# A router on rows that are not yet normed, its norm and modulation folded into its weights

## The chip, the cores and the metric

One core of one Trainium2 chip. The time is device microseconds of one execution. PE is TensorE, DVE is VectorE, ACT is ScalarE, POOL is GpSimd, SP is the queue that issues most loads.

## The reference, cut to what matters

Two layers of a hybrid block (retention, dilated attention, a gated MLP) run first, then one second block on the same 256 tokens of width 1024: a state-space mixer beside a pooling branch, then a mixture of 32 experts of hidden size 512. What the change touches is the seam between mixer and experts:

```python
xl = post_norm(xl, mod_l[2] * out_l, ln1_g, ln1_b)   # layer_norm(ALPHA * x + y) * g + b
hl = modulate(xl, mod_l[3], mod_l[4])                # x * (1 + scale) + shift
lg = hl @ w_rg + b_rg                                # 4 groups; softmax, argmax
le = hl @ w_re + b_re                                # 8 experts in each; top 2 of the group
y  = sum over the 2 experts of weight * (silu(h @ wg) * (h @ wu)) @ wd
xl = post_norm(xl, mod_l[5] * y, ln2_g, ln2_b)
```

All of it is float32.

## The kernel before

Five instruction streams are written out by hand, one for each engine and one for SP; they are tied by semaphores through `at(key)` (wait) and `then(..., key)` (signal). The operations are recorded by helpers, so all products have line 143, turns (transposes) 145, activations 147, tensor_tensor 149, tensor_scalar 151, scalar_tensor_tensor (`stt`) 153, reductions 155, copies 159, bn_stats 165, bn_aggr 167, DMAs 169.

*Up to the router.* Products of the mixer use split operands: each fp32 operand is written as a rounded high and low part (type fp32r), and three rounded products (`mm3`) take the place of one fp32 product. The output product `o2` is done for token tile 0 first, then tile 1 (128 tokens each). `first_norm(i)` on DVE scales the two halves of 512 columns by `MG[:, 1]`, adds `ALPHA * X`, takes bn_stats, and calls `layer_norm`: mean and variance, POOL takes the root, DVE subtracts and scales into `X`, multiplies by the norm's gain row `GB[:, 0]`, and DVE and POOL add the bias row `GB[:, 1]`, a half each, writing `X` in an order in which column 4p + k stands at 128k + p (`in_fours`, `by_four`). The two rows are loaded by POOL (`norm_rows`), behind its last work of the mixer.

*The router.* PE turns `X` (four 128 x 128 blocks for each `hm(i, q)`), ACT (and DVE for one quarter) applies the modulation while copying into `HM`, and PE multiplies by `WR`, 36 columns (4 groups, 32 experts), in plain fp32. DVE adds the biases, finds greatest values and one-hot rows in a chain of small instructions up to `SEL`; `CW` holds the two weights of each token, `RK` its rank within each expert (a product with a triangle), `cnt` the greatest count, from which further rounds are decided.

*The experts.* They are taken two at a time, 16 pairs, 64 places for each expert of a pair. For pair p: `ones_of(p)` on DVE makes a one-hot `ONE` (token to place) and its weighted twin `PW`; `gather` multiplies rows of `X` by `ONE` into `HG`, with the modulation applied by DVE and ACT; two parts of gate/up products (fp32, 64 columns of weights, two experts side by side in the array); `AV = silu * up`; turns; `down` products; DVE scales by `MG[:, 0]` into `OE`; and `combine(p)`, which runs on PE between the two parts of gate/up of pair p + 1, multiplies the turned `PW` by `OE` in four fp32 products of 512 columns, which DVE adds to `YA`. Pair 0's addition also takes in `ALPHA * X`.

*The loads.* Each pair needs six loads of 2 MB (gate, up, down of two experts), numbered 0 to 95. There are nine slots; loads 0 to 7 are issued by ACT during the mixer's end, load 8 (its slot overlies the norm rows) by SP once the norm is over, and load k waits on SP until the products that read load k - 9 are done:

```python
y.wait_ge(*(at("gu", r, b, i // 2) if i < 4 else at("oe", r, b, 1)))
expert_load(y, r, k)
```

## Time and profile before

| | us |
|---|---|
| median of 3 runs | 1711.09 (1708.34 to 1715.6) |
| the profiled execution | 1707.69 |
| its span | 1705.8 |
| PE busy in the span | 1627.1 (95%) |
| DVE, ACT, POOL busy | 779.8, 584.7, 468.0 |
| mean granted clock of PE | 0.982 of full |
| moved by DMA | 397.84 MB, 233 GB/s over the span |

Busy time is a sum over stages with different limits: the experts' stage begins near 1224 us of the span and has another balance of products and loads than what is ahead of it. The rows below are read stage by stage. A granted clock of 1.00 is 2.4 GHz, 0.50 is 1.2 GHz. An fp32 product is recorded as two records, a rounded one as one.

### The profile page before, as it was taken

How to read it: one execution, taken by the hardware profiler on the slowest of the kernel's cores; microseconds unless marked ns; L12 is line 12 of the kernel's file. 1: busy time of each engine (PE TensorE's matmuls, PEld its weight loads, DVE VectorE, ACT ScalarE, POOL GpSimd, SP SyncE). 2: the span in 40 equal slices, each digit the busy share in tenths (PEclk: the TensorE clock that was granted, in tenths of full speed). 3: DMA queues.
4: the chain of work that ended last, by engine and by line, in shares of the span. 5: the costliest groups of instructions: out<-in, count | busy, mean ns of one | idle time of the engine just before them, and what ended most of it. 6: DMA issues, size and time to landing. Idle time of an engine off the chain costs nothing.

```text
span 1705.8 us, 23942 instructions
## 1 busy us (share of the span) xinstructions
PE 1627.1 (95%) x9717; PEld 1214.9 (71%) x9717; DVE 779.8 (46%) x1320; ACT 584.7 (34%) x1046; POOL 468.0 (27%) x297
## 2 busy tenths in 40 slices
PE   7999999999999999999999999998699999999996
PEld 5888998878879998888777888996444434344442
DVE  5644333246563332478856665455533323233224
ACT  4543444334443343555436565332200000000000
POOL 4532545433334444300035565343000000000000
PEclk9999999999999999999999999999699999999998
DMA  7644896536439886423213344956499999999992
GB/s 259 206 135 133 253 266 213 184 119 200 141 91 300 249 250 228 127 77 99 75 50 100 101 108 135 297 170 260 166 415 421 424 421 421 424 422 425 421 424 119
DMA packets 244196, 397.84 MB, mean 233 GB/s; under 512 B 6661, under 2 KB 195521, under 8 KB 223216
## 3 DMA queue, kind: packets, MB, share of 16 engines
q1 hardware_dynamic: 237360, 365.45, 61.6%
q10 hardware_dynamic: 3760, 20.85, 3.1%
q0 software_dynamic: 2960, 9.94, 1.7%
q8 instruction: 80, 1.31, 0.3%
q14 instruction: 36, 0.29, 0.1%
HBM read 395.16 MB, written 1.05 MB: 232 GB/s over the span
## 4 chain that ended last, share of the span: by engine, by line
PE 86%; DVE 7%; issue 3%; DMA 2%; POOL 2%; ACT 1%; ACTq 0%; DVEq 0%; POOLq 0%
PE ps L143 84%; DVE arena L153 2%; PE ps L145 2%; DVE arena L149 1%; DVE split_r L149 1%; DMA rows<-in_ln_b 1%; POOL split_r L149 1%; POOL small L169 1%; DMA ring<-in_w_in 1%; DMA X<-in_x 0%; ACT split_r L147 0%; ACT arena L147 0%; DVE X L153 0%; DVE arena L159 0%; POOL arena_r L149 0%
## 5 line engine op out<-in xcount | busy, mean ns | idle before, releaser
L143 PE MATMUL ps<-arena_r,split_r 128*128 128x256 f32 (+1 forms) x2984 | 462.2, 289 | 3.7 <-POOL split_r L149 3.7
L149 POOL TENSOR_TENSOR split_r<-ring,split_r 128x1024 fp32r<-128x1024 f32 (+1 forms) x142 | 334.6, 2358 | 330.0 <-ACT split_r L147 308.0
L143 PEld LDWEIGHTS ps<-arena_r,split_r 128*128 128x128 f32 x2984 | 395.7, 189 | 20.9 <-issue 15.7
L147 ACT ACTIVATE split_r<-ring 128x1024 fp32r<-128x1024 f32 (+1 forms) x293 | 296.0, 1019 | 301.7 <-PE ps L143 216.9
L143 PE MATMUL ps<-arena 128*64 128x512 f32 (+7 forms) x1472 | 359.5, 491 | 4.7 <-DVE arena L153 2.2
L149 DVE TENSOR_TENSOR split_r<-ring,split_r 128x1024 fp32r<-128x1024 f32 (+1 forms) x151 | 212.3, 1408 | 312.8 <-ACT split_r L147 305.0
L143 PE MATMUL ps<-split_r,arena_r 128*128 128x512 f32 (+1 forms) x1520 | 342.5, 378 | 2.7 <-issue 1.7
L143 PEld LDWEIGHTS ps<-split_r,arena_r 128*128 128x128 f32 x1520 | 274.7, 188 | 51.4 <-issue 7.5
L143 PEld LDWEIGHTS ps<-arena 128*64 128x64 f32 (+2 forms) x1472 | 153.5, 156 | 164.9 <-issue 147.4
L143 PE MATMUL ps<-hhh_r,split_r 128*128 128x256 f32 (+1 forms) x976 | 222.9, 317 | 0.0
L143 PE MATMUL ps<-ring,arena 128*64 128x512 f32 (+2 forms) x768 | 214.7, 584 | 4.4 <-DVE arena L149 2.4
L147 ACT ACTIVATE arena<-ps 128x256 f32<-128x256 f32 (+4 forms) x182 | 76.6, 435 | 335.3 <-PE ps L143 330.1
L149 DVE TENSOR_TENSOR arena<-arena,ps 128x512 f32<-128x512 f32 (+1 forms) x124 | 79.4, 640 | 235.3 <-PE ps L143 200.4
L143 PEld LDWEIGHTS ps<-hhh_r,split_r 128*128 128x128 f32 x976 | 163.1, 190 | 12.2 <-issue 0.7
L143 PEld LDWEIGHTS ps<-ring,arena 128*64 128x64 f32 (+1 forms) x768 | 76.4, 145 | 108.0 <-issue 96.5
L169 POOL DMA_DIRECT2D rows<-in_ln_g x2 | 1.2, 608 | 452.8 <-PE ps L143 452.8
L147 ACT ACTIVATE arena<-ps,modc 128x128 f32<-128x128 f32 x92 | 34.5, 457 | 248.0 <-PE ps L143 218.5
L149 DVE TENSOR_TENSOR arena<-ps,rows 128x512 f32<-128x512 f32 x60 | 40.7, 690 | 138.0 <-PE ps L143 137.5
L143 PEld LDWEIGHTS ps<-arena,X 128*128 128x128 f32 x640 | 77.3, 198 | 27.3 <-issue 23.8
L143 PE MATMUL ps<-arena,X 128*128 128x128 f32 x640 | 82.6, 284 | 13.5 <-DVE arena L151 13.5
L149 POOL TENSOR_TENSOR arena_r<-arena,arena_r 128x256 fp32r<-128x256 f32 (+1 forms) x46 | 38.2, 832 | 163.5 <-ACT arena_r L147 155.0
L153 DVE SCALAR_TENSOR_TENSOR arena<-ps,rows,arena 128x508 f32<-128x508 f32 (+4 forms) x104 | 69.7, 675 | 27.0 <-ACT arena L147 20.6
(147 smaller groups left out, 1164.5 us busy)
## 6 DMA issues: line engine op xcount, KB each, us to landing
ring<-in_w_gate_up SPq DMA_DIRECT2D x88, 512.0 KB, 7.4
arena<-in_w_expert_up SPq DMA_DIRECT2D x15, 2048.0 KB, 20.5
arena<-in_w_expert_gate SPq DMA_DIRECT2D x15, 2048.0 KB, 19.7
ring<-in_w_expert_down SPq DMA_DIRECT2D x15, 2048.0 KB, 21.8
ring<-in_w_in SPq DMA_DIRECT2D x57, 512.0 KB, 5.2
ring<-in_w_expert_gate SPq DMA_DIRECT2D x13, 2048.0 KB, 18.2
arena<-in_w_ada SPq DMA_DIRECT2D x24, 1024.0 KB, 7.4
ring<-in_w_down SPq DMA_DIRECT2D x22, 1024.0 KB, 5.0
```

What stands on the lines that cost most here:

```text
L143: made = e.matmul(*a, **k)
L145: made = e.transpose(*a, **k)
L147: made = e.activation(*a, **k)
L149: made = e.tensor_tensor(*a, **k)
L153: made = e.scalar_tensor_tensor(**k)
L169: made = e.dma_start(*a, **k)
```

## The change

The router works on `LT`, the sum before its norm, and the norm's mean and root come in afterwards, through the identity logits = rstd * (LT @ W') - mean * rstd * (column sums of W') + the rest, with W' = gain * (1 + scale) * W.

- PE: 16 products of 36 columns between `projected(1)` and `state_sum(3)` make the two constant rows `SC`, from the folded columns `mul = (1 + scale) * gain` and `add = shift + (1 + scale) * bias`, which DVE prepares at m = 12 of the convolution; DVE then stores `SC` and scales `WR`.
- `first_norm` writes `LT` in the order of fours and signals each half (`r`); PE turns it as soon as it is there, ACT copies without modulation, the logits of a tile have a bank of their own. ACT writes the normed rows (without gain and bias) into `X`; the modulation behind the gathering uses the folded columns.
- `layer_norm` goes from both engines. The gain and bias rows are loaded by POOL after `o2(1)` into `GROW` and `BROW`; POOL's `residual(i)` makes the residual's rows in `YA` after the first gathering, and pair 0's addition uses them.
- In the chain of small instructions, what waits for E4's exponential is moved behind `SEL`; the rank keeps its + 1 (the one-hot compares with 1 to 64); the rank's products are two instead of three; count and `cnt` come after the first gathering.
- In each pair: `PW` goes. PE turns `ONE` and gets the weight of each place by four fp32 products with one column; ACT copies them to `ONET` (rounded) and `WSL`. DVE multiplies the down products by `WSL` and `MG` at once into `OE`, ACT rounds that to `OEH`, DVE subtracts to `OEL`, and `combine` is two rounded products for each of the four fp32 ones. `OE` has one buffer.
- SP issues load 8 after `o2(1, 1)` has been read.

The diff, with the indentation cut and without unchanged lines (the block from `Q4` to `ex0` is moved as it is):

```diff
@@ -496,6 +496,10 @@
+GROW, BROW = [view(a, 1, D)[:, 0, :] for a in (5120, 7168)]
+GCOL, BCOL, NMR = stat[:, 192:200], stat[:, 228:236], stat[:, 236:238]
+SC = small[:, 0:72]
@@ -504,18 +508,19 @@
-PW = view(3584, 2, 2, 128)
...
-PWT = view(9728, 2, 256)
+ONET = view(9728, 2, 256, rounded=True)
+OEL, OEH = [view(a, 1, D, rounded=True)[:, 0, :] for a in (6144, 7168)]
+WSL = stat[:, 190:192]
...
-SEL, RK, CW, RS, CM = R(400, 2, 32), R(464, 2, 32), R(528, 2, 32), R(592, 2, 32), R(656, 1, 2)
+SEL, RK, CW, RS, CM, CB = R(400, 2, 32), R(464, 2, 32), R(528, 2, 32), R(592, 2, 32), R(656, 1, 2), R(660, 2, 36)
@@ -961,6 +966,13 @@
+        bk = take(("sc",), ("sc", "kept"))
+        t.wait_ge(*at("ab"))
+        t.wait_ge(s_small[5], 32)
+        t.wait_ge(s_small[6], 128)
+        for o, column in ((0, modc_mul), (36, modc_add)):
+            made = summed(bk[:, o:o + 36], [(column(24 + k, 1, 0).to_broadcast([P, P]), WR[:, k, :]) for k in range(8)])
+        made.then_inc(*sig(s_mm, ("sc",)))
@@ -1168,26 +1180,25 @@
-        bkl = take(("lg",), ("lg", "kept"), hold=True)
...
-                for h in range(2):
-                    t.wait_ge(*at("ln", 1, i, h))
+                t.wait_ge(*at("r", i, q))
...
-                    made = t.transpose(bk[:, tok(k)], X[:, i, tok(4 * q + k)], ident)
+                    made = t.transpose(bk[:, tok(k)], LT[i][:, tok(4 * q + k)], ident)
...
-            t.wait_ge(s_small[5], 32)
-            t.wait_ge(s_small[6], 128)
+            t.wait_ge(*at("wr"))
+            bk = take(("lg", i), ("lg", i, "kept"))
...
-                made = t.matmul(bkl[:, i * 36:i * 36 + 36], HM[:, k, tok(i)], WR[:, k, :], k == 0, k == 7)
+                made = t.matmul(bk[:, 0:36], HM[:, k, tok(i)], WR[:, k, :], k == 0, k == 7)
...
-        drop(("lg",))
...
-        summed(bk[:, 0:32], [(C("tlt"), SEL[:, 0, :])])
-        summed(bk[:, 32:64], [(C("tlt"), SEL[:, 1, :]), (ones, SEL[:, 0, :])]).then_inc(*sig(s_mm, ("rk",)))
+        t.matmul(bk[:, 0:64], C("tlt"), SEL.rearrange("p t n -> p (t n)"), True, False)
+        t.matmul(bk[:, 32:64], ones, SEL[:, 0, :], False, True).then_inc(*sig(s_mm, ("rk",)))
+    def counts():
@@ -1204,9 +1215,11 @@
-            t.wait_ge(*at("pwd", r, p))
...
-                made = t.transpose(bk[:, tok(x)], PW[:, i, x, :], ident)
+                t.transpose(bk[:, tok(x)], ONE[:, i, x, :], ident)
+            for e in range(2):
+                c = slice(64 * e, 64 * e + 64)
+                made = summed(bk[c, 256:257], [(ONE[:, i, x, c], CW[:, x, 2 * p + e:2 * p + e + 1]) for x in range(2)])
@@ -1250,12 +1263,18 @@
-                t.wait_ge(*at("oe", r, p, h, "kept"))
+                t.wait_ge(*at("oeh", r, p, h))
+                t.wait_ge(*at("oel", r, p, h))
...
-                t.matmul(bk, PWT[:, i, tok(x)], OE[:, i, half(h)], True, True).then_inc(*sig(s_done, ("ya", r, p, h, x)))
+                t.matmul(bk, ONET[:, i, tok(x)], OEH[:, half(h)], True, False)
+                t.matmul(bk, ONET[:, i, tok(x)], OEL[:, half(h)], False, True).then_inc(*sig(s_done, ("ya", r, p, h, x)))
+        for i in range(2):
+            t.wait_ge(*at("n", i))
...
+        if r == 0:
+            counts()
@@ -1693,13 +1712,10 @@
-                if q or i == 0:
-                    s.wait_ge(*at("hm", i, q))
-                    for k in range(4):
-                        f = 24 + 4 * q + k
-                        made = s.activation(HM[:, 4 * q + k, tok(i)], B("hm", i, q)[:, tok(k)], ACT.Identity,
-                                            scale=modc_mul(f, 1, 0), bias=modc_add(f, 1, 0))
-                    made.then_inc(*sig(s_act, ("hm", i, q, "kept")))
+                s.wait_ge(*at("hm", i, q))
+                s.activation(HM[:, 4 * q:4 * q + 4, tok(i)], fold(B("hm", i, q), 4), ACT.Copy).then_inc(*sig(s_act, ("hm", i, q, "kept")))
+            s.wait_ge(*at("nm", i))
+            s.activation(X[:, i, :], LT[i], ACT.Identity, scale=RV[:, i:i + 1], bias=NMR[:, i:i + 1]).then_inc(*sig(s_act, ("n", i)))
@@ -1719,7 +1735,8 @@
-            s.activation(PWT[:, i, :], B("pw", r, p)[:, 0:256], ACT.Copy).then_inc(*sig(s_done, ("pw", r, p, "kept")))
+            s.activation(ONET[:, i, :], B("pw", r, p)[:, 0:256], ACT.Copy)
+            s.activation(WSL[:, i:i + 1], B("pw", r, p)[:, 256:257], ACT.Copy).then_inc(*sig(s_done, ("pw", r, p, "kept")))
@@ -1729,6 +1746,11 @@
+            for h in range(2):
+                s.wait_ge(*at("oe", r, p, h, "kept"))
+                if r == 0 and p == 0:
+                    s.wait_ge(*at("residual", 1))
+                s.activation(OEH[:, half(h)], OE[:, 0, half(h)], ACT.Copy).then_inc(*sig(s_done, ("oeh", r, p, h)))
@@ -2217,6 +2239,14 @@
+            if m == 12:
+                v.wait_ge(*at("bp_in"))
+                add, mul = modc[:, 24:32, 0], modc[:, 32:40, 0]
+                then(v.tensor_tensor(BCOL, BCOL, mul, ALU.mult))
+                then(v.tensor_tensor(mul, mul, GCOL, ALU.mult))
+                v.wait_ge(*v.latest)
+                then(v.tensor_tensor(add, add, BCOL, ALU.add), ("ab",))
@@ -2274,6 +2304,12 @@
+        v.wait_ge(*at("sc"))
+        v.wait_ge(*at("rbg_in"))
+        v.wait_ge(*at("rbe_in"))
+        v.copy(SC[:, 0:36], B("sc")[:, 0:36])
+        then(v.tensor_tensor(SC[:, 36:72], B("sc")[:, 36:72], small[:, R_RB:R_RB + 36], ALU.add), ("sc", "kept"))
+        then(v.tensor_tensor(WR, WR, bc(modc_mul(24, 8, 0), 36), ALU.mult), ("wr",))
@@ -2343,48 +2379,35 @@
-    def layer_norm(name, tiles, x):
-        i0, i1 = tiles[0], tiles[-1] + 1
-        for i in tiles:
...
-            then(v.bn_aggr(MV[:, i, :], BN[:, i, :, :]))
...
-        then(v.tensor_scalar(RV[:, i0:i1], MV[:, i0:i1, 1], 1e-5, None, ALU.add), ("var", name, i0))
-        v.wait_ge(*at("rstd", name, i0))
-        for i in tiles:
-            then(v.tensor_scalar(x[:, i, :], x[:, i, :], MV[:, i, 0:1], RV[:, i:i + 1], ALU.subtract, ALU.mult))
-            v.wait_ge(*at("ln_row", name, 0))
...
-            for h in range(2):
-                then(v.tensor_tensor(LT[i][:, half(h)], x[:, i, half(h)], GB[:, 0, half(h)], ALU.mult), ("lng", name, i, h))
-            v.wait_ge(*at("ln_row", name, 1))
...
-            then(v.tensor_tensor(in_fours(x[:, i, half(1)]), by_four(LT[i][:, half(1)]), by_four(GB[:, 1, half(1)]), ALU.add), ("ln", name, i, 1))
...
-            then(v.stt(X[:, i, half(h)], X[:, i, half(h)], ALPHA, PT1[:, h, :], ALU.mult, ALU.add))
...
-            then(v.bn_stats(BN[:, i, h, :], X[:, i, half(h)]))
-        layer_norm(1, [i], X)
+            then(v.stt(in_fours(LT[i][:, half(h)]), by_four(X[:, i, half(h)]), ALPHA, by_four(PT1[:, h, :]), ALU.mult, ALU.add), ("r", i, h))
+        for h in range(2):
+            v.wait_ge(*at("r", i, h))
+            then(v.bn_stats(BN[:, i, h, :], LT[i][:, half(h)]))
+        v.wait_ge(*v.latest)
+        then(v.bn_aggr(MV[:, i, :], BN[:, i, :, :]))
+        v.wait_ge(*v.latest)
+        then(v.tensor_scalar(RV[:, i:i + 1], MV[:, i, 1:2], 1e-5, None, ALU.add), ("var", 1, i))
+        v.wait_ge(*at("rstd", 1, i))
+        then(v.stt(NMR[:, i:i + 1], MV[:, i, 0:1], -1.0, RV[:, i:i + 1], ALU.mult, ALU.mult), ("nm", i))
...
-        v.wait_ge(*at("hm", 1, 0))
-        c = tok(1)
-        then(v.tensor_tensor(HM[:, 0:4, c], fold(B("hm", 1, 0), 4), bc(modc_mul(24, 4, 0), P), ALU.mult))
...
-        then(v.tensor_tensor(HM[:, 0:4, c], HM[:, 0:4, c], bc(modc_add(24, 4, 0), P), ALU.add), ("hm", 1, 0, "kept"))
-        v.wait_ge(*at("lg", 1))
-        v.wait_ge(*at("rbg_in"))
-        v.wait_ge(*at("rbe_in"))
-        then(v.tensor_tensor(LG, fold(B("lg")[:, 0:72], 2), small[:, R_RB:R_RB + 36].unsqueeze(1).to_broadcast([P, 2, 36]), ALU.add), ("lg", "kept"))
+        for i in range(2):
+            v.wait_ge(*at("nm", i))
+            then(v.stt(CB[:, i, :], SC[:, 0:36], NMR[:, i:i + 1], SC[:, 36:72], ALU.mult, ALU.add))
+        for i in range(2):
+            v.wait_ge(*at("lg", i))
+            v.wait_ge(*v.latest)
+            then(v.stt(LG[:, i, :], B("lg", i)[:, 0:36], RV[:, i:i + 1], CB[:, i, :], ALU.mult, ALU.add), ("lg", i, "kept"))
@@ -2399,31 +2422,31 @@
+        then(v.tensor_tensor(Q4, LG[:, :, 0:4], bc(M0, 4), ALU.is_ge))
...
+        then(v.tensor_tensor(EX, M2, M1, ALU.subtract), ("ex0",))
...
-        then(v.tensor_tensor(Q4, LG[:, :, 0:4], bc(M0, 4), ALU.is_ge))
...
-        then(v.tensor_tensor(EX, M2, M1, ALU.subtract), ("ex0",))
@@ -2439,8 +2462,8 @@
-        v.wait_ge(*v.latest)
-        then(v.tensor_scalar(RK, RK, -1.0, None, ALU.add))
+    def counted():
@@ -2477,19 +2500,12 @@
-                v.wait_ge(*at("hg", r, p - 2, 1))
-            for x in range(2):
-                for e in range(2):
-                    k = 2 * p + e
-                    made = v.tensor_scalar(ONE[:, i, x, 64 * e:64 * e + 64], iota[:, 0:64], rank[:, x, k:k + 1], None, ALU.is_equal)
-            then(made, ("one", r, p))
-            if p >= 2:
...
-                    made = v.tensor_scalar(PW[:, i, x, 64 * e:64 * e + 64], iota[:, 0:64], rank[:, x, k:k + 1], CW[:, x, k:k + 1], ALU.is_equal, ALU.mult)
-            then(made, ("pwd", r, p))
+                    made = v.tensor_scalar(ONE[:, i, x, 64 * e:64 * e + 64], iota[:, 1:65], rank[:, x, k:k + 1], None, ALU.is_equal)
+            then(made, ("one", r, p))
@@ -2507,7 +2523,8 @@
-                        then(v.stt(by_four(y), in_fours(X[:, x, half(h)]), ALPHA, by_four(bk), ALU.mult, ALU.add), ("ya", r, p, h, x, "kept"))
+                        v.wait_ge(*at("residual", x))
+                        then(v.stt(y, y, ALPHA, bk, ALU.mult, ALU.add), ("ya", r, p, h, x, "kept"))
@@ -2518,6 +2535,8 @@
+        if r == 0:
+            counted()
@@ -2537,9 +2556,13 @@
-                if p >= 2:
-                    v.wait_ge(*at("ya", r, p - 2, 1, 1))
-                then(v.tensor_tensor(OE[:, i, half(h)], B("oe", r, p, h), MG[:, 0, half(h)], ALU.mult), ("oe", r, p, h, "kept"))
+                v.wait_ge(*at("pw", r, p, "kept"))
+                if p:
+                    v.wait_ge(*at("ya", r, p - 1, 1, 1))
+                then(v.stt(OE[:, 0, half(h)], B("oe", r, p, h), WSL[:, i:i + 1], MG[:, 0, half(h)], ALU.mult, ALU.mult), ("oe", r, p, h, "kept"))
+            for h in range(2):
+                v.wait_ge(*at("oeh", r, p, h))
+                then(v.tensor_tensor(OEL[:, half(h)], OE[:, 0, half(h)], OEH[:, half(h)], ALU.subtract), ("oel", r, p, h))
@@ -2706,17 +2729,21 @@
-    def layer_norm(name, tiles, x):
-        i0, i1 = tiles[0], tiles[-1] + 1
-        power(RV[:, i0:i1], i1 - i0, ("var", name, i0), ("rstd", name, i0))
-        for i in tiles:
-            g.wait_ge(*at("ln_row", name, 1))
-            g.wait_ge(*at("lng", name, i, 0))
-            then(g.tensor_tensor(in_fours(x[:, i, half(0)]), by_four(LT[i][:, half(0)]), by_four(GB[:, 1, half(0)]), ALU.add), ("ln", name, i, 0))
-    def norm_rows(name, a, b):
+    def norm_rows(name, a, b, rows):
...
-            g.dma_start(GB[:, k, :], A[n][0].partition_broadcast(P)).then_inc(*landed(s_row[k], ("ln_row", name, k)))
+            g.dma_start(rows[k], A[n][0].partition_broadcast(P)).then_inc(*landed(s_row[k], ("ln_row", name, k)))
+    def residual(i):
+        for k in range(2):
+            g.wait_ge(*at("ln_row", 1, k))
+        g.wait_ge(*at("n", i))
+        for h in range(2):
+            then(g.tensor_tensor(by_four(YA[:, i, half(h)]), in_fours(X[:, i, half(h)]), by_four(GROW[:, half(h)]), ALU.mult))
+        g.wait_ge(*g.latest)
+        for h in range(2):
+            made = g.tensor_tensor(YA[:, i, half(h)], YA[:, i, half(h)], BROW[:, half(h)], ALU.add)
+        then(made, ("residual", i))
@@ -2728,6 +2755,8 @@
+    for o, name in ((GCOL, "ln1_g_2"), (BCOL, "ln1_b_2")):
+        g.dma_start(fold(o, 2), A[name][0].rearrange("(q p k) -> p q k", q=2, k=4)).then_inc(*landed(s_col[3]))
@@ -2774,15 +2803,16 @@
-    g.wait_ge(*at("ga", 3, 1, 0))
-    g.wait_ge(*at("silu", 23))
-    for m in range(20, 24):
-        g.wait_ge(*at("tk", m))
-    norm_rows(1, "ln1_g_2", "ln1_b_2")
...
-        layer_norm(1, [i], X)
+        power(RV[:, i:i + 1], 1, ("var", 1, i), ("rstd", 1, i))
+        if i == 0:
+            g.wait_ge(*at("o2", 1))
+            norm_rows(1, "ln1_g_2", "ln1_b_2", (GROW, BROW))
+    g.wait_ge(*at("hg", 0, 0, 0, "kept"))
+    for i in range(2):
+        residual(i)
...
-    norm_rows(2, "ln2_g_2", "ln2_b_2")
+    norm_rows(2, "ln2_g_2", "ln2_b_2", (GB[:, 0, :], GB[:, 1, :]))
@@ -2850,8 +2880,7 @@
-    y.wait_ge(*at("ln", 1, 1, 0))
-    y.wait_ge(*at("ln", 1, 1, 1))
+    y.wait_ge(*at("o2", 1, 1, "kept"))
```

## Rows read from the trace of the kernel before

**Rows 1.** The page's strip of GB/s moved, 40 equal slices of 42.6 us.

```profile
GB/s 259 206 135 133 253 266 213 184 119 200 141 91 300 249 250 228 127 77 99 75 50 100 101 108 135 297 170 260 166 415 421 424 421 421 424 422 425 421 424 119
```

**Rows 2.** Windows: length, busy time by engine, granted clock, DMA share, GB/s.

```profile
1192.00:1193.00 1.00, 0.00 (x0) 0.00 (x0) 0.43 (x1) 0.00 (x0) 0.00 (x0) 0.67 1.16 492
1200.00:1210.00 10.00, 6.90 (x32) 6.16 (x30) 7.82 (x12) 2.90 (x8) 2.21 (x2) 0.50 0.69 268
1400.00:1500.00 100.00, 100.00 (x480) 41.71 (x478) 30.29 (x66) 7.73 (x19) 0.00 (x0) 1.00 1.01 422
```

**Rows 3.** The chain that ended last, 1140 to 1270: start, length, what.

```profile
1180.29 17.11 DMA rows<-in_ln_b
...
1214.46 0.24 DVE arena L149
...
1215.13 0.22 ACT arena L147
```

**Rows 4.** Timeline, 1155 to 1232: start, length, engine, instruction, count, idle before.

```profile
1165.12 14.21 PE L143 MATMUL ps<-split_r,arena_r 128*128 128x512 f32 x60
...
1179.86 8.67 PE L143 MATMUL ps<-split_r,arena_r 128*128 128x512 f32 x36 [0.53 <-POOL split_r L149]
...
1182.95 0.69 DVE L153 SCALAR_TENSOR_TENSOR arena<-ps,rows 128x512 f32<-128x512 f32 x1 [2.15 <-PE ps L143]
...
1187.66 0.56 POOL L149 TENSOR_TENSOR stat<-stat,negh 128x1 f32<-128x1 f32 x1 [6.84 <-DVE stat L151]
...
1197.42 1.04 DVE L149 TENSOR_TENSOR X<-arena,rows 128x512 f32<-128x512 f32 x1 [4.98 <-DMA rows<-in_ln_b]
1197.46 2.02 POOL L149 TENSOR_TENSOR X<-arena,rows 128x512 f32<-128x512 f32 x1 [9.24 <-DMA rows<-in_ln_b]
...
1208.20 1.94 PE L145 MATMUL ps<-cst_sb,X 128*128 128x128 f32 x8 [2.26 <-DVE X L149]
...
1210.80 3.63 PE L143 MATMUL ps<-small,arena 128*128 128x36 f32 x16 [0.65 <-DVE arena L149]
...
1219.46 0.56 DVE L149 TENSOR_TENSOR arena<-arena 128x64 f32<-128x64 f32 x3
...
1223.59 5.20 PE L143 MATMUL ps<-arena,X 128*128 128x128 f32 x32 [1.25 <-DVE arena L151]
...
1228.93 3.65 PE L143 MATMUL ps<-arena 128*64 128x512 f32 x16
```

**Rows 5.** Timeline, 866 to 925, TensorE at the state sums.

```profile
884.78 0.28 PE L143 MATMUL ps<-hhh_r,split_r 128*128 128x256 f32 x1
...
886.48 7.97 PE L143 MATMUL ps<-arena 128*128 128x512 f32 x20 [1.41 <-DVE arena L149]
```

**Rows 6.** Timeline, 1228 to 1290: gate and up of two pairs, a combination.

```profile
1247.24 13.95 PE L143 MATMUL ps<-ring,arena 128*64 128x512 f32 x64
...
1261.12 3.70 PE L143 MATMUL ps<-arena 128*128 128x512 f32 x8
...
1276.19 7.51 PE L143 MATMUL ps<-arena 128*64 128x512 f32 x33
```

**Rows 7.** SP's queue: issues of loads 9 and 95; us to landing (last column).

```profile
1236.06 0.37 SPq L169 DMA_DIRECT2D arena<-in_w_expert_up  x1
...
arena<-in_w_expert_up SPq DMA_DIRECT2D x1, 2048.0 KB, 9.2
...
1648.31 0.34 SPq L169 DMA_DIRECT2D ring<-in_w_expert_down  x1
...
ring<-in_w_expert_down SPq DMA_DIRECT2D x1, 2048.0 KB, 28.0
```

**Rows 8.** Timeline, 1640 to 1706: the last pair's down products and around them.

```profile
1677.34 1.03 DVE L149 TENSOR_TENSOR arena<-arena,ps 128x512 f32<-128x512 f32 x1 [6.41 <-PE ps L143]
...
1679.86 8.78 PE L143 MATMUL ps<-ring,arena 128*64 128x512 f32 x32 [0.79 <-DVE arena L159]
...
1689.74 0.69 DVE L149 TENSOR_TENSOR arena<-arena,ps 128x512 f32<-128x512 f32 x1 [0.35 <-PE ps L143]
```

14 lines of the change are left out of this document (4 added, 10 removed).

## The prediction

> **What bounds the kernel now.** I read the per-slice strips first, then the windows, then the chain that ended last, then the timeline at the places that the change touches. The strip of GB/s [rows 1] says that from the 29th slice on (about 1,236 us) the transfers never pause. The window 1400 to 1500 [rows 2] shows both at once: PE busy 100 of 100 us, and DMA share 1.01 at 422 GB/s. So which one sets the end has to be worked out. A pair of experts takes PE 1276.19 - 1247.24 = 28.95 us [rows 6]. It also takes six loads of 2.097 MB. At 422 GB/s that is 6 x 4.97 = 29.8 us. PE is therefore a little faster than its loads already, and lives on the nine slots filled beforehand. The last two rows of the queue say how much of that lead is left: load 95, issued at 1648.31, lands 28.0 us later, at 1676.3 [rows 7], and the products that need it start at 1679.86 [rows 8]. The lead is 3.5 us. Anything that makes PE faster in this stage is worth 3.5 us and no more; what is worth its full price is whatever starts the stream of loads earlier. That stream starts when the first half of the first pair's gate/up products has freed two slots: issue at 1236.06 [rows 7]. From there to the landing of load 95 are 440.2 us, which the transfers fix.
>
> What comes before it is a serial stretch. The chain [rows 3] holds 17.11 us of waiting for the norm's two rows from memory, until 1197.39; the logits are added at 1214.46, gathering begins at 1223.59 and the experts' products at 1228.93 [rows 4].
>
> **Before the router (a loss).** The 16 products for `SC` are placed on PE after `projected(1)`, ahead of `state_sum(3)`. Router products of the same 36 columns took 3.63 us for 16 records at half clock [rows 4], 0.227 each, so 0.113 at full clock; 16 fp32 products are 32 records, 3.6 us. PE idles 1.41 us at this spot, for DVE [rows 5], so 2.1 to 2.2 us come on top, and PE has hardly a pause afterwards to take them up in. I take +2.1; bounds 0 (a later wait for a load absorbs it) and 3.6. The new DVE work (three tiny ones at m = 12, two of 36 columns and one of 288 before `gated(0)`, together under 1.2 us by the 0.2 us of small DVE instructions) lies beside PE's eight state records and twelve first scan records, 7.97 us [rows 5]; uncovered it would cost 1. Two more small DMAs on POOL's queue near the start lie ahead of a load whose reader comes much later: at nothing, 1.6 us if it did not.
>
> **Rows to logits.** No product waits for norm rows now. Output products of tile 0 are read by DVE at 1182.95, tile 1's end at about 1188.5 [rows 4]. Tile 0: two halves of 0.69 (scale) and 1.04 (sum, written permuted; the permuted write of that size took 1.04), two bn_stats of 0.7, two small ones, POOL's root 0.56, one small: done near 1189.5. Tile 1 the same from there: rows ready at 1193.0, `nm` at 1196.0, `CB` at 1196.5. POOL issues its two row loads (0.6 each) between the two roots, beside DVE's work. PE in its order: turns of tile 0 at 1188.6, its logits after ACT's copies (0.6 each, after 0.9 of issues) from 1190.1, turns of tile 1, its logits. At full clock the last logits are there at 1195.5 and DVE's chain decides: the first reduction at 1197.1 instead of 1214.73. At half clock PE decides: logits 3.6 us each (just that price stands in [rows 4]), turns 0.97 for four, which comes to 1199.6, reduction at 1200.1. PE stopped at 1188.5, and the clock fell in the window 1192 to 1193 [rows 2]; here PE is busy about half the time, so I take the middle: 16.2 us earlier, bounds 14.6 and 17.6. ACT's normed rows for `X` (1.1 us each) lie beside this and are needed only at the gathering.
>
> **Logits to gathering.** E4's exponential leaves the chain: ACT's 0.22 [rows 3], two hand-overs and two DVE instructions under 0.2 each, of which one was beside nothing: -0.5. From the end of `SEL` (about 1220.0) to the gathering are 3.6 us today [rows 4]. E4's two DVE instructions now lie in there (+0.4), but RK - 1, the wait for the count, its reduction and its cast (four steps, 0.9) go behind the gathering: -0.5.
>
> **Gathering to first products.** 5.34 us today [rows 4]. New on PE: four one-column fp32 products (8 records) and the count's four records. By the 0.113 of small records that is 1.3; bounds 0.5 and 2.7 (all at half clock). So gate/up starts, and the stream with it, 16.2 + 0.5 + 0.5 - 1.3 - 2.1 = 13.8 us earlier. The ninth load, now tied to `o2(1,1)` and not to the norm, lands before and fits into DMA time that stands empty today.
>
> **In the expert stage.** Combining today: four fp32 products of 512 columns, 3.70 us [rows 6]. Then: eight rounded ones. Rounded products of 512 columns took 14.21 / 60 = 0.237 [rows 4], so 1.9 with gaps: -1.75. Added 8 records, 0.9. PE's pair takes 28.1 us; fifteen pairs save it 13, but 29.8 us of loads per pair stay. The Trainium skill (DMA: Bandwidth & Descriptors, Where 436 GB/s comes from) gives a ceiling of 435 GB/s for transfers into SBUF; this case's 422 is near it, so no faster stream is to be hoped for. By the page's number the 86 loads behind the first would take an estimated 415 us in place of the 431 that the rows show; the trace is used.
> DVE gains two subtractions of 0.7 and loses four small ones of 0.2; ACT gains two casts of 0.6 and a tiny copy. Both stand idle most of a pair. The combine of pair p-1 starts 6.9 us after its down products end; OE, OEH and OEL take 2.3 of these. POOL's residual (eight instructions, 2.02 us for a permuted one [rows 4], so at most 16 us) starts at about 1214 and is wanted by OEH of pair 0 near 1240; without that cover it would be paid in full.
> With the loads deciding, load 93 lands 10 us before load 95 (two times 5); 7.2 us of gate/up products and 2.5 us from AV (1677.34) to the down products (1679.86) fit in, so the last down products start with the landing and not 3.5 us behind it: -3.4.
>
> **The end.** PE waits longer before the last down products. Today half clock in part of them made 8.78 us of what is 6.9 (half of 13.95) [rows 6, 8]; I add 0.9 (0 to 1.7). Behind them DVE's first addition came 1.16 us after their end (1689.74 [rows 8] against 1688.6); now OE of the second half, its cast, two subtractions and two products stand before it, 2.3 us: +1.1.
>
> **Sum.** -13.8 - 3.4 + 0.9 + 1.1 = -15.2 us. The profiled execution took 1707.69 us (span 1705.8), 3.4 below the median of 1711.09; it would take 1692.5, and the median 1695.9. The bounds of the costs together, not all at one end, make it -19 to -11: 1692 to 1700.
>
> **Rivals.**
> (a) *PE still decides.* If the loads went faster as PE asks for them sooner, PE's 13 us would show too: -13.8 - 13 + 1.1 = -26, 1685. Against it: a share of 1.01 in every window of the stage, and latencies that grow from 9.2 to 28.0 us [rows 7], which is a backlog in the transfers and not in the requests. Chance 0.05.
> (b) *The front gains less.* The added products upstream knock on (3.6 and another microsecond or two where the clock falls), and the router runs at half clock throughout: 13.8 becomes 8 to 10, the sum -10, 1701. For it: the window 1200 to 1210 ran at half clock throughout, busy though PE was for 6.9 of the 10 us [rows 2]. Chance 0.2, a third of it within 0.5%.
> (c) *Clock lost to waits for loads.* PE now pauses about 1.7 us per pair once its lead is gone. A pause of about 3 us before the last down products cost 1.9 us of clock [rows 8]. If each pause did, PE's pair would be 28.1 + 1.9 = 30.0, just over the loads' 29.8: 6 pairs by 0.2, 1 us more, and 3 us if it is worse at the end: 1697 to 1699. The Trainium skill (TensorE: Matmul & The Clock Gate, HAM oscillation) warns that waits for DMA between bursts drag the clock down and up again. The loss limits itself, since a slower PE no longer waits. Chance 0.1.
> (d) *Slower: the one-column products are dear.* They hit PE in every pair, four of them. The sum comes to zero when a pair takes PE 29.7 us, that is when 8 records cost 2.5 us, 0.31 each; at 0.38 it is 0.5% slower, 1720. For it: I found no product with one column in this stretch to price it by, and each changes its weights. Against it: small records with full weight loads took 0.113 at full and 0.227 at half clock. Chance 0.03. That rounded products on these tiles go at the fp32 price would add 3.4 us to each pair (some 45 us slower): no row speaks for it, 0.01.
> (e) *It does not start earlier.* Something else holds the first pair, such as the slots 4 to 8 landing late: they are in by about 1211 today and are wanted after 1222. Then only the 3.4 less 2 of the tail are left, no change. Chance 0.03.
>
> **How the numbers follow.** The forecast has 0.58, at 1695.9, own range 1692 to 1700. With (b) and (c) on the high side, and (a) partly on the low one, 1689 to 1703 holds 8 in 10. 0.5% is 8.6 us, about what a measurement of this kernel can tell. Faster: 0.58 + 0.05 + 0.13 of (b) + 0.1 = 0.86. Same: 0.07 of (b) and 0.03 of (e), 0.1. Slower: both of (d), 0.04.
>
> **What would show it.** Right: no wait for `in_ln_b` in the chain; first reduction near 1200.6 (16.2 earlier, 2.1 later for the products upstream); first expert load of the stage on SP's queue near 1222; the same 440 us from it to the last landing; combine blocks of 8 records in about 1.9 us; PE idle for loads in the last six pairs or so; PE's share below 100 in the late windows at DMA 1.01. Wrong: a stretch from first issue to last landing shorter than 435 (then (a)); that issue later than 1226 (then (b) or (e), and the records at 885 and the granted clock from 1188 to 1200 say which); a PE pair over 29.8 with no wait for loads (then (d)); half clock in the middle of the stage (then (c)).

## The result, and the profile after

The changed kernel takes 1691.29 us (median of 4 runs, 1689.29 to 1692.46) against 1709.99 (4 runs, 1708.34 to 1715.6) of the kernel before: ratio 0.9888, 95% interval 0.9871 to 0.9905. Forecast were 1695.9 us and 1689 to 1703. The profiled execution took 1690.42 us, its span 1688.6, 17.2 less than the 1705.8 of before; the forecast for the span was -15.2. The median lies inside the wide range and 0.7 us below the narrow one (1692 to 1700) of the forecast.

The chain of waits that ended last, where [rows 3] had 17 us of waiting for `in_ln_b` (start, length, what):

```profile
1182.38 8.68 PE ps L143 x36
...
1192.69 1.98 PE ps L143 x16
1194.66 1.68 PE ps L145 x8
1196.35 3.48 PE ps L143 x16
...
1200.14 0.17 DVE arena L155
```

No load of the norm's rows is in it. The path goes from TensorE's output products over the turns, ACT's copy and the logits to the first reduction; the second tile's logits ran at half clock. The timeline of the same stretch and what follows, to be held against [rows 4]:

```profile
1196.18 3.63 PE L143 MATMUL ps<-small,arena 128*128 128x36 f32 x16
...
1207.54 5.79 PE L143 MATMUL ps<-arena,X 128*128 128x128 f32 x32 [1.69 <-DVE arena L151]
...
1212.83 3.00 POOL L149 TENSOR_TENSOR arena<-X,arena 128x512 f32<-128x512 f32 x2 [16.03 <-DVE arena L149]
...
1213.47 0.41 PE L143 MATMUL ps<-arena 128*64 128x1 f32 x8
1213.81 0.63 PE L143 MATMUL ps<-arena,cst_sb 128*128 128x32 f32 x4
1214.37 13.95 PE L143 MATMUL ps<-arena 128*64 128x512 f32 x64
...
1221.50 0.37 SPq L169 DMA_DIRECT2D arena<-in_w_expert_up  x1
```

The last line is load 9, the start of the stream: 14.56 us earlier than in [rows 7]. POOL's residual begins at 1212.83, and the products of pair 0's combination waited for nothing: it is hidden. Upstream, at the state sums, against [rows 5]:

```profile
887.62 3.95 PE L143 MATMUL ps<-small,modc 128*128 128x36 f32 x32
891.38 9.78 PE L143 MATMUL ps<-arena 128*128 128x512 f32 x20
905.12 0.87 PE L143 MATMUL ps<-arena 128*64 128x256 f32 x8 [2.21 <-DVE arena L153]
```

In the experts' stage the windows (length, busy time of each engine, granted clock, DMA share, GB/s) and TensorE's waits from 1400 on (us, times, longest) show what TensorE does with the work it lost, where [rows 2] had it busy 100 of 100:

```profile
1400.00:1500.00 100.00, 98.33 (x522) 44.67 (x520) 32.83 (x60) 12.99 (x31) 0.00 (x0) 1.00 1.01 423
1500.00:1600.00 100.00, 94.36 (x518) 47.05 (x514) 29.94 (x52) 11.19 (x28) 0.00 (x0) 1.00 1.01 422
```

```profile
PE ps L143 <- DMA arena<-in_w_expert_up: 5.8, 4, 3.4
PE ps L143 <- DMA ring<-in_w_expert_gate: 4.1, 4, 1.2
PE ps L143 <- DMA arena<-in_w_expert_gate: 3.3, 2, 2.3
PE ps L143 <- DMA ring<-in_w_expert_up: 1.6, 2, 0.8
```

These are 14.8 us of waits for loads in all, two for each of the last six pairs, as forecast. Two combinations, one pair apart, and the end, against [rows 6, 8]:

```profile
1412.44 2.11 PE L143 MATMUL ps<-arena_r 128*128 128x512 f32 x8
1440.05 2.11 PE L143 MATMUL ps<-arena_r 128*128 128x512 f32 x8
...
1651.83 8.78 PE L143 MATMUL ps<-arena 128*64 128x512 f32 x32 [3.37 <-DMA arena<-in_w_expert_up]
...
1663.24 7.09 PE L143 MATMUL ps<-ring,arena 128*64 128x512 f32 x32 [0.78 <-DVE arena L159]
...
1671.87 2.42 PE L143 MATMUL ps<-arena_r 128*128 128x512 f32 x8 [1.54 <-ACT arena_r L147]
1672.61 0.69 DVE L149 TENSOR_TENSOR arena<-arena,ps 128x512 f32<-128x512 f32 x1
```

TensorE's pair is down from 28.95 to 27.61 us (1440.05 - 1412.44; the forecast had 28.1), 20 us over 15 pairs, and most of it comes back as waits. What the end of the stage hangs on is load 93, the last up load. The chain that ended last shows it:

```profile
1615.46 36.23 DMA arena<-in_w_expert_up
```

It landed at 1651.69, 430.2 us behind the issue of load 9, and from there to the last down products are 11.5 us. Load 95 was issued at 1625.40:

```profile
ring<-in_w_expert_down SPq DMA_DIRECT2D x1, 2048.0 KB, 36.0
```

It landed 36.0 us later, at 1661.4, which is 439.9 us behind the issue of load 9 (forecast 440).

### The profile page after: what moved, and what is told of

Its sections match the earlier page's. It is cut to its first block, busy times and chain, and to the rows that moved or that the text cites. A ratio compares the mean times of both kernels' runs of the same rounds, so it can differ in the third digit from the quotient of the medians.

```text
span 1688.6 us, 24295 instructions
## 1 busy us (share of the span) xinstructions
PE 1608.7 (95%) x9875; PEld 1227.5 (73%) x9875; DVE 779.1 (46%) x1288; ACT 605.9 (36%) x1088; POOL 476.1 (28%) x305
## 4 chain that ended last, share of the span: by engine, by line
PE 78%; DMA 10%; DVE 7%; POOL 2%; issue 2%; ACT 1%; ACTq 0%; DVEq 0%; POOLq 0%; SPq 0%
PE ps L143 77%; DMA arena<-in_w_expert_up 4%; DMA ring<-in_w_expert_gate 4%; DVE arena L153 2%; PE ps L145 2%; DVE split_r L149 1%; DVE arena L149 1%; DMA ring<-in_w_out 1%; POOL split_r L149 1%; ACT split_r L147 1%; POOL small L169 1%; DMA ring<-in_w_in 1%; DMA X<-in_x 1%; DVE arena_r L149 0%; ACT arena L147 0%
## 5 line engine op out<-in xcount | busy, mean ns | idle before, releaser
L143 PE MATMUL ps<-arena 128*64 128x512 f32 (+8 forms) x1472 | 310.2, 458 | 12.8 <-DMA arena<-in_w_expert_up 4.2
L143 PEld LDWEIGHTS ps<-arena 128*64 128x64 f32 (+2 forms) x1472 | 138.2, 151 | 136.1 <-issue 120.0
L149 DVE TENSOR_TENSOR arena<-arena,ps 128x512 f32<-128x512 f32 (+1 forms) x124 | 75.5, 637 | 222.4 <-PE ps L143 186.8
L147 ACT ACTIVATE arena<-ps 128x256 f32<-128x256 f32 (+4 forms) x170 | 72.5, 442 | 258.0 <-PE ps L143 239.6
L147 ACT ACTIVATE arena_r<-arena 128x512 fp32r<-128x512 f32 (+2 forms) x98 | 52.3, 542 | 153.2 <-DVE arena L153 110.4
L147 ACT ACTIVATE arena<-ps,modc 128x128 f32<-128x128 f32 x80 | 30.0, 455 | 201.0 <-PE ps L143 200.5
```

Of the source, the lines that this page charges most:

```text
L143: made = e.matmul(*a, **k)
L147: made = e.activation(*a, **k)
L149: made = e.tensor_tensor(*a, **k)
```

## The experiments

Twelve kernels, measured in three groups (e1, e2, e5, e6; e3, e4, e7, e8; e9 to e12); each group has its own runs of the kernel before (medians 1710.37, 1709.49 and 1709.16). To read them I divide each profile's span at three places: the start of `o2`'s second half of products (1179.86 in [rows 4]), the issue of load 9, and the start of the last down products.

| kernel | median | o2 | o2 to load 9 | load 9 to last down | last down to end |
|---|---|---|---|---|---|
| before | 1709.99 | 1179.86 | 56.20 | 443.80 | 25.94 |
| changed | 1691.29 | 1182.38 | 39.12 | 441.74 | 25.36 |
| e1 front part alone | 1690.1 | 1180.75 | 37.31 | 443.80 | 24.04 |
| e2 expert part alone | 1710.47 | 1186.12 | 57.94 | 442.54 | 27.20 |
| e3 combination twice | 1702.24 | 1186.18 | 39.13 | 450.76 | 27.53 |
| e4 half of the down loads | 1677.09 | 1185.50 | 37.32 | 423.56 | 27.22 |
| e5 SC moved | 1686.44 | 1178.77 | 37.50 | 441.77 | 25.46 |
| e6 rows early | 1705.12 | 1187.26 | 51.50 | 443.80 | 25.84 |
| e7 loads in halves | 1685.07 | 1177.28 | 34.48 | 442.30 | 25.54 |
| e8 halves, front alone | 1689.47 | 1182.72 | 33.28 | 447.24 | 24.26 |
| e9 halves at the ends | 1687.42 | 1183.29 | 34.08 | 441.20 | 27.03 |
| e10 changed, again | 1690.94 | 1179.95 | 37.79 | 441.69 | 25.47 |
| e11 SC moved, again | 1692.12 | 1180.78 | 39.24 | 441.67 | 25.51 |
| e12 front alone, again | 1692.89 | 1186.73 | 36.75 | 443.80 | 24.02 |

(Differences of profile rows; one execution each. In e7 to e9 "load 9" is its first half, some 3.4 us earlier by design.) The third column of differences (load 9 to last down) repeats to 0.1 us in kernels with the same expert stage (e2 is the exception, 0.8 us longer: its last up products took 9.82 us for 8.78). The one before it (`o2` to load 9) lies within 2.5 us for kernels with the same front, mostly by the router's clock; `o2` itself scatters over 7 us where the work is the same. So stages are compared by their columns, and totals by medians.

**e1 and e2: the two parts apart.** e1 is the changed kernel with the expert stage of before:

```diff
-ONET = view(9728, 2, 256, rounded=True)
-OEL, OEH = [view(a, 1, D, rounded=True)[:, 0, :] for a in (6144, 7168)]
...
+PWT = view(9728, 2, 256)
...
-t.matmul(bk, ONET[:, i, tok(x)], OEH[:, half(h)], True, False)
-t.matmul(bk, ONET[:, i, tok(x)], OEL[:, half(h)], False, True)
+t.matmul(bk, PWT[:, i, tok(x)], OE[:, i, half(h)], True, True)
```

e2 is the kernel before with that part of the change and nothing else.

> The router's part of the change alone: the experts' stage is that of the kernel before (weighted one-hot PW, four fp32 products in a combination, two buffers of OE). If the load stream decides and its start is what was gained: issue of load 9 some 14.5 us earlier than before, 440 us from there to the landing of load 95, last down products 3.5 us behind it as before; 14 to 15 us faster than before, so 3 to 4 us slower than the full change. If PE's lighter pairs made a good part of the gain: clearly less than 12 us.

> The experts' part alone, on the kernel before: one-hot turned, weights as a column, combination in rounded products. If the load stream decides: PE's pair falls from 28.95 to 27.6 us but PE waits for loads at the end; the lead of 3.5 us less 1.2 us of longer tail, give or take 1.7 us of clock: 1 to 4 us faster. If PE decides: 15 times 1.35, about 19 us faster.

Measured: e1 1690.1 us, ratio 0.9883 (0.9865 to 0.9901), e12 (the same kernel again) 1692.89, ratio 0.9898 (0.9884 to 0.9912); e2 1710.47, ratio 0.9995 (0.9981 to 1.0009). The front part alone gives what the whole change gives. The expert part alone gives nothing that can be seen; I had expected 1 to 4 us, and the interval reaches from 3.2 us faster to 1.5 slower. Its stage column is 1.26 us shorter than before and its end 1.26 us longer. e1 came out better than I expected of it: I had it 3 to 4 us behind the full change. The window 1400 to 1500 of e1, and its timeline:

```profile
1400.00:1500.00 100.00, 100.00 (x502) 43.53 (x502) 31.07 (x67) 8.90 (x23) 0.00 (x0) 1.00 1.01 424
```

```profile
1218.06 0.37 SPq L169 DMA_DIRECT2D arena<-in_w_expert_up  x1
...
1661.86 7.09 PE L143 MATMUL ps<-ring,arena 128*64 128x512 f32 x32 [0.78 <-DVE arena L159]
```

From load 9 to the last down products it takes 443.80 us, the same to the hundredth as the kernel before, whose stage it has. The end is shorter than in [rows 8] because the last down products ran at full clock, 7.09 us for 8.78.

**e3: the combination's products twice.**

```diff
+t.matmul(bk, ONET[:, i, tok(x)], OEH[:, half(h)], True, False)
+t.matmul(bk, ONET[:, i, tok(x)], OEL[:, half(h)], False, True)
 t.matmul(bk, ONET[:, i, tok(x)], OEH[:, half(h)], True, False)
...
```

> The changed kernel, with the two rounded products of each quarter of a combination issued twice (the sum is made over with the same operands, the result is the same). That is 8 more records of 512 columns in each pair, 1.9 to 2.1 us by the 2.12 us that 8 of them took in the changed kernel: TensorE's pair goes from 27.6 to about 29.6 us. Theory (the loads decide, 29.8 us a pair): the waits for loads, 14.8 us in all in the changed kernel, shrink to next to nothing and the time stays, 0 to +2 us. Rival (TensorE's work shows in the time): +28 us or more.

Measured 1702.24 us (1701.22 to 1705.39), ratio 0.995 (0.9933 to 0.9966): 11 us slower than the changed kernel, neither 2 nor 28. By the columns 9.0 of them lie in the stage and 2.2 at the end.

```profile
1309.44 3.92 PE L143 MATMUL ps<-arena_r 128*128 128x512 f32 x16
...
1338.87 3.92 PE L143 MATMUL ps<-arena_r 128*128 128x512 f32 x16
...
1676.07 8.78 PE L143 MATMUL ps<-ring,arena 128*64 128x512 f32 x32 [0.78 <-DVE arena L159]
```

The pair takes 29.43 us (1338.87 - 1309.44), below the 29.8 of its loads, and still TensorE waits for no load and decides. The theory had compared pair with pair. But between load 9 and the last down products TensorE has 15 pairs and some 9.6 us to do. The 9.6 is what the kernel before leaves over (443.80 - 15 x 28.95); with it, 15 x 29.43 + 9.6 = 451.1 here, for 450.76 measured. The loads' side does not go by 15 pairs: from load 9 to the landing of load 93 it is 85 loads (430.2 us in the changed kernel), then come 11.5 us of products and of the steps between them, together 441.7. So the two cross at about (441.7 - 9.6) / 15 = 28.8 us a pair, not at 29.8.

**e4: half of each down weight loaded.** The down products read the second half of their rows from what the slot held before; TensorE's work stays the same.

```diff
-o, src = slot_for(r, k), w.rearrange("(p k) n -> p (k n)", k=4)
+o, src = slot_for(r, k)[:, 0:2048], w.rearrange("(p k) n -> p (k n)", k=4)[:, 0:2048]
```

> The changed kernel, with only the first half of each partition's rows of the down weights loaded (the other half of the slot holds what was there, so the output of the experts is not the reference's). Six loads of a pair carry 10.5 MB instead of 12.6, 24.8 us instead of 29.8 at 422 GB/s; TensorE's work is the same. Theory (the loads decide in the changed kernel): TensorE's 14.8 us of waits for loads vanish and its pair of 27.6 us decides; 13 to 15 us faster than the changed kernel, about 1677. Rival (TensorE or the chain between products decides already): no change, within 2 us.

Measured 1677.09 us (1671.9 to 1681.79), ratio 0.9807 (0.9777 to 0.9837), 14 us faster than the changed kernel. No wait for a load is left, and TensorE's 15 x 27.61 + 9.6 = 423.8 is what the third column of times shows (423.56): 18 us less than the loads leave it in the changed kernel. There, then, the loads decide. Two combinations of e4, for its pair of 27.61 us:

```profile
1303.33 2.11 PE L143 MATMUL ps<-arena_r 128*128 128x512 f32 x8
...
1330.94 2.11 PE L143 MATMUL ps<-arena_r 128*128 128x512 f32 x8
```

**e5: the SC products elsewhere**, at m = 9 of the convolution, ahead of `dt_sums`, with DVE's part in front of them.

```diff
 if m == 9:
+    bk = take(("sc",), ("sc", "kept"))
...
+    made.then_inc(*sig(s_mm, ("sc",)))
     dt_sums()
```

> The full change with the 16 products for SC (and DVE's work on them) moved ahead of the dt sums at m = 9, where PE idled 3.9 us for DVE. If the cost of these products upstream (4.1 us by the trace: 2.2 of their own and 1.8 of half clock behind them) reaches the end: 4 us faster than the full change, 21 to 23 faster than before. If the later waits for the w_out loads take it up (the delay was 5.8 us at 1088 and 2.5 us at 1182): 0 to 2 us faster than the full change.

Measured 1686.44 us (1685.33 to 1692.99) and, as e11 beside e10, 1692.12 (1688.97 to 1693.63) against 1690.94. The first looked like a gain of 5 us; the second says none. All runs pooled: 1689.8 (mean of 8, standard error 1.2) against 1691.2 (mean of 10, 1.1) for the changed kernel. Not told apart from nothing. The timeline and the windows at the new place show why it should be little: the clock falls there too, and what follows the products runs at half of it.

```profile
782.42 3.66 PE L143 MATMUL ps<-small,modc 128*128 128x36 f32 x32
786.36 4.73 PE L143 MATMUL ps<-arena,cst_sb 128*128 128x32 f32 x24 [0.28 <-DVE arena L149]
```

```profile
786.00:788.00 2.00, 1.72 (x12) 1.64 (x11) 1.97 (x4) 1.67 (x2) 0.00 (x0) 0.76 1.10 324
788.00:790.00 2.00, 2.00 (x11) 2.00 (x11) 1.64 (x4) 0.00 (x0) 0.00 (x0) 0.50 0.58 142
```

**e6: the kernel before, with the norm's rows loaded early.** `norm_rows` stands ahead of POOL's work on the last branches; the rows are issued at 1061 us.

```diff
 squares(15)
+g.wait_ge(*at("ga", 3, 1, 0))
...
+norm_rows(1, "ln1_g_2", "ln1_b_2")
 for n in range(8):
...
-g.wait_ge(*at("ga", 3, 1, 0))
...
-norm_rows(1, "ln1_g_2", "ln1_b_2")
 for i in range(2):
     layer_norm(1, [i], X)
```

> The kernel before with its two norm rows loaded by POOL before the u products (nothing else changed). If the wait for the rows held DVE for its full length in the trace (1189.1 to 1197.4): 8 us faster than before, so about half of the change's gain. If the rows only hid other waits (POOL's root, the order of the tiles): under 4 us.

Measured 1705.12 us (1702.45 to 1710.34), ratio 0.997 (0.9958 to 0.9983). The wait of 17.11 us in [rows 3] is gone and `o2` to load 9 is 4.70 us shorter, where I had expected 8. Its timeline shows why: the first tile's turns still wait for the norm itself (4.10 us, for its normed rows), and the second tile's work, which used to be done under the wait, now stands in line.

```profile
1201.56 1.60 PE L145 MATMUL ps<-cst_sb,X 128*128 128x128 f32 x8 [4.10 <-DVE X L149]
...
1210.84 1.94 PE L145 MATMUL ps<-cst_sb,X 128*128 128x128 f32 x8 [3.24 <-DVE X L149]
...
1217.37 0.16 DVE L155 TENSOR_REDUCE arena<-arena 128x2 f32<-128x8 f32 x1
```

One thing in this profile is not the edit's. Its output products ran in part at half clock, where those of the kernel before had 1.00 throughout; they took 10.20 us for 8.67, and DVE's first read came 4.61 us behind `o2` and not 3.09:

```profile
1187.26 10.20 PE L143 MATMUL ps<-split_r,arena_r 128*128 128x512 f32 x36 [2.04 <-POOL split_r L149]
```

```profile
1188.00:1190.00 2.00, 2.00 (x7) 1.54 (x6) 0.20 (x1) 0.00 (x0) 0.00 (x0) 0.57 0.98 414
```

So of the 17.1 us that the change gains between `o2` and the first reduction, 4.8 (34.87 less 30.11 here) were to be had by an earlier load, 6.3 if the 1.5 us of clock are taken out. The other 11 to 12 are what is left for taking the norm out of the path; that is a difference, and no run shows it by itself.

**e7, e8, e9: can the expert part be made to pay?** If the loads decide, what starts the stream earlier counts. Each load is issued in two halves (1 MB), released and awaited by halves of the products; e7 does it to the full change with SC moved, e8 to the front part alone, e9 to the full change only for loads 9, 10 and 92 to 95.

```diff
+if k == 3:
+    made.then_inc(*sig(s_done, ("guh", r, p, part)))
...
+y.wait_ge(*(at("gu", 0, b, i // 2) if q else at("guh", 0, b, i // 2)))
+expert_load(y, 0, k, q)
```

> The kernel with the SC products moved (1686.4 us), in which every expert load from the ninth on is issued in two halves of 1 MB, each released by the half of the products that read its place, and waited for by the half that needs it. The stream starts after half of the first gate products, 3.5 us earlier; at the end the last up products start with the first half of the last up weights and are over 3.5 us behind the landing and not 7.1 behind it. Theory (what counts is when the stream starts and what stands behind its end, TensorE has slack): -3.5 - 3.6 = -7 us, about 1679.5. Rival (TensorE decides): 0 to -1. Another rival: halves of 8 KB for each partition move slower, or the requests are too many; then the rate falls under 415 GB/s and it is slower.

> The same halves and the moved SC products, on the kernel that has the front part alone (the expert stage of before, whose pair takes TensorE 28.95 us without a wait for a load). Theory (there TensorE decides, with a lead of 3.5 us over the loads): an earlier start of the stream only makes that lead longer, so only the moved SC products count, 2 to 4 us against the 1690.1 of the front part alone: 1686 to 1688, and 6 to 8 us behind the full change with halves. So the expert part, worth nothing until now, is worth 6 to 8 us here. Rival (the loads decide in both): it is as fast as the full change with halves, within 2 us.

> The full change with the SC products moved, in halves only where halves help: the first two loads of the stream (9 and 10) and the last four (92 to 95); the 81 loads between stay whole. In the profile of the kernel with all loads in halves the stream started 3.4 us earlier, but the rate was 420 instead of 422 to 423 GB/s, about 2 us over the stream, and the last up products started with the first half of load 93, 2.4 us ahead of its landing. Theory (start and end of the stream count at full price, the rate comes back with whole loads): load 93 lands 3.4 us earlier than with whole loads, the last up products start another 2.4 us earlier: 5.8 us faster than the kernel with the SC products moved, measured beside it. Rival (the rate was a chance of that run, TensorE is next to decide): as the kernel with all loads in halves, 1 to 3 us faster than the one with the SC products moved.

Measured: e7 1685.07 us (1681.35 to 1692.13), ratio 0.9865 (0.9838 to 0.9893); e8 1689.47 (1688.37 to 1690.9), ratio 0.9878 (0.9862 to 0.9895); e9 1687.42 (1682.81 to 1692.35), ratio 0.9873 (0.9856 to 0.989), beside 1690.94 and 1692.12 of e10 and e11. The window 1400 to 1500 of e7, its timeline, and that of e8:

```profile
1400.00:1500.00 100.00, 100.00 (x537) 46.09 (x534) 32.52 (x60) 12.33 (x29) 0.00 (x0) 1.00 1.01 420
```

```profile
1215.19 0.33 SPq L169 DMA_DIRECT2D arena<-in_w_expert_up  x1
...
1642.64 8.78 PE L143 MATMUL ps<-arena 128*64 128x512 f32 x32 [3.40 <-DMA arena<-in_w_expert_up]
...
1654.06 7.14 PE L143 MATMUL ps<-ring,arena 128*64 128x512 f32 x32 [0.78 <-DVE arena L159]
```

```profile
1663.24 7.09 PE L143 MATMUL ps<-ring,arena 128*64 128x512 f32 x32 [0.78 <-DVE arena L159]
```

In e8 the earlier start gave nothing, as expected, though the total missed: 1689.47 where I had 1686 to 1688, and 4.4 us behind e7 where I had 6 to 8. Counted from the second half's issue (1219.44), the stage takes 443.80 us once more. In e7 it takes 438.87 from there (1215.19), 2.9 less than the 441.7 of whole loads, and not the 3.4 + 3.6 that I expected: the rate was 420 GB/s for 422 to 423, which is 2 us over the stream, and at the end 2.4 us were won at most; 0.9 stay open. In e9, with whole loads between,

```profile
1638.12 8.76 PE L143 MATMUL ps<-arena 128*64 128x512 f32 x32 [2.24 <-DMA arena<-in_w_expert_gate]
...
1648.84 7.09 PE L143 MATMUL ps<-arena 128*64 128x512 f32 x32
...
1658.57 8.77 PE L143 MATMUL ps<-ring,arena 128*64 128x512 f32 x32 [0.78 <-DVE arena L159]
```

it takes 437.76 from the second half's issue at 1220.81, 4.0 less than whole loads; 1.8 of the expected 5.8 is missing, since the last up products now stand behind TensorE's own work (no wait in front of 1648.84), whose gate part ran slowly after a wait. Behind the stage, the last down products lost 1.7 more to the clock. Nine runs of e7 and e9 together: mean 1686.8 (standard error 1.3), against 1691.2 (1.1) for ten of the changed kernel. The halves with SC moved are the best version that I have, 4.4 us faster than the changed kernel with an uncertainty (95%) of 3.3. Against the kernel with SC moved alone (1689.8, eight runs) the halves are 3.0 us faster with an uncertainty of 3.5: the stage column shows their gain, the totals do not yet. The same holds for e7 against e8. Their means are 3.6 us apart with an uncertainty of 4.8; the columns, counted from the second half's issue, say 4.9 in the stage less 1.3 at the end. So with halves the expert part is worth some 3.6 us by the profiles, which the totals bear out only weakly.

**e10, e12: changed kernel and front part alone, once more** (e11 stands with e5).

> The changed kernel once more, unaltered, as the one to compare with on this chip: 1689 to 1693 us. What the profiles of eight kernels with the same work up to the last branch differ in there, up to 8 us, is taken for chance; if that is so, its runs spread over several microseconds.

> The kernel with the SC products moved once more, unaltered, beside the changed kernel. Local reading: at the spot between the projection and the state sums the changed kernel spends 4.1 us more than the kernel before; at the new spot the products and the low clock behind them cost about as much. So theory: 0 to 2 us faster than the changed kernel. Rival (the first measurement shows an effect): 4 to 5 us faster.

> The front part alone once more, unaltered, beside the changed kernel. Theory: the expert part swaps one limit (TensorE, 443.8 us from the issue of load 9 to the last down products) for another (the loads, 441.7) and adds 1.2 us behind the last down products: the changed kernel is 0.9 us faster than this one, within 2 us of it either way. Rival (the expert part is worth the 3.4 us of the prediction and more): 3 us or more slower than the changed kernel.

e10 1690.94 us (1686.47 to 1697.76, 6 runs), ratio 0.99 (0.9881 to 0.9918); with the first runs, ten of the changed kernel have mean 1691.2 (1.1) and eight of the front part alone 1691.1 (0.8). The difference is 0.1 with an uncertainty of 2.7. The stage columns say that the changed kernel should gain 0.7 (2.1 in the stage, less 1.4 at the end); that is too little to be seen.

## Why the prediction was right, point by point

The time lay in the range and near the forecast: -17.2 us in the profile's span for -15.2 predicted, and the ratio 0.9888 makes it -19.2 (-22 to -16). So the gain was larger than the 15.2 forecast, by a little more than the noise. The mechanism held: no wait for the norm's rows, a stream that starts earlier, loads that decide. That the sum came within 2 us of the span is in part luck: the stage gave 1.3 us less than forecast, the clock at the end 2.6 more, and the work ahead of `o2`, +2.5 in this profile, scatters over 7 us.

- **SC products, +2.1.** The products took 3.95 us where 3.6 were set, but the clock fell behind them: the state sums took 9.78 us instead of 7.97. From the end of the projection to 905.12 the changed kernel needs 17.56 us, before it was 13.35 [rows 5]: +4.2 at the spot. That term was half of what it is locally. The moved SC products bear this out: the state sums took 7.97 us in all profiles without the SC products in front of them (before, e2, e5 to e9, e11) and 9.65 to 11.29 in the six with them. Of the whole upstream stretch, +2.52 in this profile, nothing can be said: kernels with the same work there begin `o2` anywhere between 1179.95 and 1186.73.
- **Rows to logits, -16.2 (14.6 to 17.6).** -17.11: from `o2` to the first reduction 34.87 became 17.76. In eight other profiles with this front (e1, e4, e5, e7 to e10, e12) it was 15.73 to 15.75, in e1 with both tiles' logits at full clock (1.98 and 1.97 us); the change is worth -19.1 there. In e3 and e11 it was 17.8 again, with the second tile at half clock. At full clock I was 1.5 us too late (17.6 for 19.1); my other end, both tiles at half clock, occurred in no profile. That the clock in the router decides over 2 us was right.
- **Logits to gathering, -1.0; gathering to products, +1.3.** -1.46 and +1.49. Of the second, 0.90 us are the new products (8 one-column records 0.41 us, counts 0.63, overlapping a little), for the 1.3 forecast; the other 0.59 are the gathering, which ran slower (5.79 us for 5.20).
- **Start of the stream, -13.8.** -14.56, of which the last step (7.13 us from the first products to the issue) is unchanged.
- **In the stage, -3.4.** -2.06. The step "the last down products start with the landing" failed: load 95 landed at 1661.4, but they started at 1663.24. What ends last is load 93: the last up products start with its landing at 1651.83 and, after 3.37 us of waiting, take 8.78 us instead of 7.09. I had set 7.2 us of products and 2.5 us of steps against 10 us between the landings of loads 93 and 95; it was 11.4 us against 9.7. The clock term of the end had the right size at the wrong products.
- **The end, +0.9 and +1.1.** -1.69 (the down products at full clock) and +1.18.
- **Sum.** -14.56 - 2.06 - 1.69 + 1.18 - 0.07 = -17.2.

*The rivals.* (a) is out: 439.9 us from first issue to last landing, and e4 shows that TensorE would need 18 us less than the loads give it. (b) held for one tile's logits and for the local price of SC, and was made up for by the rest. (c): the waits for loads in the changed kernel's stage, up to 1.2 us in the two windows, left the granted clock there at 1.00, and the products behind the one of 2.28 us later on took 7.09 us, the time of full clock; only the 3.37 us before the last up products cost 1.7 us. The Trainium skill (TensorE: Matmul & The Clock Gate, HAM oscillation) describes such a loss in every tile; here it came at the end alone. The length of the pause does not settle it: in e9 the products behind a wait of 2.24 us took 8.76 us. And the last down products, which the prediction took as its example, stand behind the same two short waits (1.20 and 0.78 us) in the kernel before, where they took 8.78 us, and in e1, e8 and e12, where they took 7.09. What decides was not looked for. But the step by which I priced (c) was wrong: it held TensorE's pair against "the loads' 29.8". By e3 the level is 28.8, and a pair of 30.0 would have cost 1.2 us each time and not 0.2. (d): 8 records cost 0.41 us, against the 2.5 at which the gain would have been gone; that price was rightly worked out from TensorE's own 28.95, and e3 bears it out (29.43 us a pair took back 9 of the changed kernel's gain in the stage). (e): slots 4 to 8 were never waited for.

*What the change is worth where.* All of the gain that can be seen is the front's (e1), but 1.7 us of it are the clock of the last down products in e1's profile. Of the 17 to 19 us between `o2` and load 9, some 5 to 6 would have come from loading the norm's rows earlier (e6); the rest, 11 to 14, is left for routing on rows not yet normed. The expert part takes 20 us of work from TensorE and returns about 0.7: the kernel before sat just 2.1 us above the level of its loads.

## What to carry to other kernels

When an engine and the transfers are both busy without a pause, work out what each has to do between the same two events, ends included, and not per period: 29.4 us a pair lost here against 29.8 us of loads, because one side had 15 pairs and 9.6 us to do, and the other 85 loads (a little over 14 pairs) and the 11.5 us behind the last of them. Once the stream decides, only its start and what stands behind its end have their full price, and smaller first pieces can start it earlier. Where a wait for a load seems to cost 17 us, ask what is done under it: removing it alone gave 5 to 6.
